# Moving the end of VectorE's order in the dense expert loop: gates ahead of rows in the last 16 steps

## The reference

```python
top_s, top_pos = lax.top_k(cand_s, PEER_TOPK)
experts = jnp.take_along_axis(cand_i, top_pos, axis=-1)
g = jax.nn.softmax(top_s, axis=-1)
u = peer_u[experts]
act = jax.nn.gelu(jnp.einsum('thkd,td->thk', u, xb), approximate=False)
v = peer_v[experts]
return jnp.einsum('thk,thkd->td', g * act, v)
...
y = layer_norm(ALPHA * h + ff, ln2_g, ln2_b)
```

## Time and profile before

| | us |
|---|---|
| median of 3 runs | 3522.22 |
| lowest and highest run | 3514.46, 3530.64 |
| profiled execution, its own time | 3518.77 |
| its span in the profile | 3517.0 |
| PE busy | 3031.8 |
| VectorE busy | 2456.1 |
| ScalarE busy | 1205.2 |
| GpSimd busy | 1549.8 |

### The profile page before, as it was taken

How to read it: one execution, slowest core, us unless ns; L and a number is a source line. 1 busy time by engine, 2 the same in 40 slices (tenths; PEclk the granted TensorE clock), 3 DMA queues, 4 the chain that set the end, 5 groups by cost and what they waited for, 6 DMA issues and landing times. The chain is left out here.

```text
span 3517.0 us, 36218 instructions
## 1 busy us (share of the span) xinstructions
PE 3031.8 (86%) x10170; PEld 1718.4 (49%) x10170; DVE 2456.1 (70%) x5185; ACT 1205.2 (34%) x3180; POOL 1549.8 (44%) x1186
## 2 busy tenths in 40 slices
PE   8979989776889896776886899999998999999996
PEld 5755745444645453444653554444444444444442
DVE  0122068887786878877767677888878888788887
ACT  0241233665543435764552322222222222222221
POOL 0000035567562288888777533233333333334331
PEclk9989999886799998886697999999999999999998
DMA  4665589666699997576578999999999999999996
GB/s 145 210 252 187 173 325 375 235 194 202 215 340 374 336 347 232 150 197 173 168 252 295 404 411 394 410 403 406 406 398 397 414 407 402 384 411 415 408 401 245
DMA packets 375914, 1098.52 MB, mean 312 GB/s; under 512 B 91713, under 2 KB 210209, under 8 KB 289569
## 3 DMA queue, kind: packets, MB, share of 16 engines
q0 software_dynamic: 165072, 751.05, 57.1%
q1 hardware_dynamic: 176800, 303.85, 24.6%
q10 hardware_dynamic: 33840, 41.30, 3.3%
HBM read 1031.97 MB, written 63.02 MB: 311 GB/s over the span
## 5 line engine op out<-in xcount | busy, mean ns | idle before, releaser
L428 POOL DMA_INDIRECT expert_rows<-in_experts,picked_index x640 | 769.6, 1202 | 1254.7 <-DVE ff_sum L583 1142.6
L571 DVE SCALAR_TENSOR_TENSOR expert_rows<-expert_rows,h_tile 128x1024 f32<-128x1024 f32 x672 | 819.2, 1219 | 244.6 <-DMA expert_rows<-in_experts,picked_index 218.1
L583 DVE SCALAR_TENSOR_TENSOR ff_sum<-expert_rows,coefficients,ff_sum 128x1024 f32<-128x1024 f32 x672 | 859.8, 1279 | 139.5 <-ACT coefficients L534 138.0
L1792 PE MATMUL dense_act_ps<-dense_hT,key_columns 128*128 128x384 f32 x2048 | 705.3, 499 | 114.5 <-DMA key_columns<-in_key_columns 103.6
L451 POOL DMA_INDIRECT gates_by_expert<-dense_gate,gate_address x384 | 673.8, 1755 | 156.7 <-issue 124.5
L1781 PE MATMUL dense_out_ps<-dense_value_rows,dense_weights 128*128 128x512 f32 x1536 | 682.5, 595 | 17.9 <-DVE dense_weights L1860 17.9
L1792 PEld LDWEIGHTS dense_act_ps<-dense_hT,key_columns 128*128 128x128 f32 x2048 | 389.1, 194 | 450.4 <-DMA key_columns<-in_key_columns 180.0
L1781 PEld LDWEIGHTS dense_out_ps<-dense_value_rows,dense_weights 128*128 128x128 f32 x1536 | 292.9, 191 | 362.5 <-issue 310.6
L839 PE MATMUL proj_ps<-xT,w_in_block 128*128 128x384 f32 (+1 forms) x1392 | 422.0, 466 | 36.1 <-PEq L1601 15.5
L839 PEld LDWEIGHTS proj_ps<-xT,w_in_block 128*128 128x128 f32 x1392 | 267.8, 193 | 189.4 <-issue 35.6
L1826 ACT ACTIVATE dense_weights<-dense_act_ps 128x384 f32<-128x384 f32 x128 | 62.6, 489 | 742.5 <-PE dense_act_ps L1792 730.9
(11 more groups left out here) (189 smaller groups left out, 3088.2 us busy)
## 6 DMA issues: line engine op xcount, KB each, us to landing
key_columns<-in_key_columns SPq DMA_DIRECT2D x128, 512.0 KB, 11.6
dense_value_rows<-in_experts SPq DMA_DIRECT2D x128, 512.0 KB, 8.2
gates_by_expert<-zeros POOLq DMA_DIRECT2D x12, 2048.0 KB, 21.9
wq_half<-in_peer_wq SPq DMA_DIRECT2D x48, 512.0 KB, 12.6
dense_gates<-gates_by_expert SPq DMA_DIRECT2D x128, 192.0 KB, 12.1
w_in_block<-in_w_in ACTq DMA_DIRECT2D x18, 1024.0 KB, 9.8
w_in_block<-in_w_in SPq DMA_DIRECT2D x18, 1024.0 KB, 8.1
w_out<-in_w_out SPq DMA_DIRECT2D x24, 512.0 KB, 7.8
```

The costliest lines, as they stand in the source:

```text
L428: pool.indirect_dma_start(to, None, self.a["experts"], bass.IndirectOffsetOnAxis(ap=index[:, k:k + 1], axis=0)).then_inc(self.got[p % self ...
L571: dve.scalar_tensor_tensor(place, place, 1.0, self.h[n % 2][:], ALU.mult, ALU.mult, accum_out=self.dots[:, s % TOPK:s % TOPK + 1]).then_in ...
L583: dve.scalar_tensor_tensor(total, self.ring[:, p % self.RING, D:2 * D], self.coef[:, y % TOPK:y % TOPK + 1], total, ALU.mult, ALU.add).the ...
L1792: mm = nc.tensor.matmul(up[it % 2][:, 0:W], keys[it % KB][:, k, :], hTd[:, k, :], start=(k == 0), stop=(k == KC - 1))
```

## The change

In the last 16 steps VectorE takes the gates earlier: `ahead` grows from 2 to 6 tiles over the steps 121 to 124 (two gates in each of them), so that the last gate stands in step 129 and not in step 133. SyncE loads the gates earlier in the same measure. And the function `part` has a larger divisor (259, before 253): in every step before 130 a smaller share of the background list is due. Step 130 takes it to 0.985, step 131 to the end (before: step 132).

```diff
-        LAG, AHEAD = 8, 2
+        LAG, CATCH_UP = 8, 16
...
-        part = lambda it: min(1.0, (min(it + 1, ET) + max(0, it + 1 - LAG)) / (2 * ET - 3))
+        ahead = lambda it: 2 + min(4, max(0, it - (ET + LAG - CATCH_UP)))
+        weighed = lambda it: min(ET, max(0, it - LAG + ahead(it) + 1))
+        part = lambda it: ((min(it + 1, ET) + max(0, it + 1 - LAG)) / (2 * ET + 3) if it < ET + LAG - 6 else
+                           0.985 if it == ET + LAG - 6 else 1.0)
...
-                e = it - LAG + 4
-                if 0 <= e < ET:
+                for e in range(weighed(it + 1), weighed(it + 2)):
                     if e == 0:
                         wait_for_scores(sp, m, len(GROUPS))
...
                     sp.dma_start(gts[e % GB][:], gates_of[e]).then_inc(gts_in[e % GB], 16)
+                e = it - LAG + 4
+                if 0 <= e < ET:
                     if e >= VB:
                         sp.wait_ge(v_filled, e - VB + 1)
                     sp.dma_start(vals[e % VB][:], table[e][:, D:2 * D]).then_inc(vals_in[e % VB], 16)
...
-                e = it - LAG + AHEAD
-                if 0 <= e < ET:
+                for e in range(weighed(it - 1), weighed(it)):
                     dve.wait_ge(gelud, e + 1)
                     dve.wait_ge(gts_in[e % GB], 16 * (e // GB + 1))
                     nc.vector.tensor_tensor(w[e % AB][:], w[e % AB][:], gts[e % GB][:], ALU.mult).then_inc(gated, 1)
```

## The result

| | before | after |
|---|---|---|
| median us | 3522.28 (4 runs) | 3566.33 (4 runs, 3563.41 to 3571.28) |
| ratio | 1 | 1.012, 95% interval 1.010 to 1.014 |
| span in the profile | 3517.0 | 3561.7 |

The change makes the kernel 44 us slower. The forecast was 3526 us, +3.5, with 3544 as the upper end of its range.

The account below looks back on a forecast made before the run. Bytes moved were taken to bound the loop, with rows tied to TensorE. Last gelu 3430, plus 46 and 44.5, gave a 3520.5 us span, +3.5 against 3517.0; median 3526, range 3508 to 3544.

Parts of the forecast that it names:

- What bounds the kernel: Dense loop: bound by bytes moved, DMA share 1.00 at 404 GB/s; VectorE's rows cannot run ahead of TensorE.
- Part 3, the gate loads: SyncE's queue, last dense steps: early gate loads could hold back key columns, but don't while VectorE is at TensorE's step.
- the 10.35 us of that part: VectorE waiting for tile 124's gelu before its gate: costs at most one TensorE step if cover is gone.
- Part 2, the divisor: Rows near the loop's end: 24 coefficients stand behind the last dense gelu, moving the last row's dot product to 3476.
- g: End of the last dense gelu on ScalarE: 3443.1 us before, forecast 3430.
- rival 1: TensorE gains nothing because keys still land in 12 us: last dense gelu stays 3443, +15.5 to +19.5 us; chance 20%.
- X - g: From last dense gelu's end (g) to start of the last row's dot product (X) on VectorE: forecast 46 us.
- byte count: Data still to move after the last dense gelu: 20.4 MB, at about 415 GB/s 49 us.
- VectorE's own chain: VectorE's remaining rows 653 to 671 and two gates after the last dense gelu: 45 us at the earliest.
- Part 1, the tail: No gates behind the last row, sample sums sooner after it: worth 3.5 us, 7.3 at most.
- End minus X: From the last row's dot product to the kernel's end: 48 us before, forecast 44.5, floor 40.7; h load kept at 8.8.
- a DMA share clearly under 1: Sign that the forecast is wrong: in the loop, fetches starved by the held rows.

Follow-up runs that it names:

- e12: Gates up to six tiles ahead, 10 gate buffers, old divisor 253, coefficients one dense gelu earlier, against the kernel before: 3505.77 us, 0.9940.
- e5: The whole change (divisor 259) with 10 gate buffers and coefficients one dense gelu earlier, against the kernel before: 3519.52 us, 0.9979.
- e3: The whole change with 10 gate buffers instead of 4, against the kernel before: 3531.77 us, 1.0027.
- e4: Gates up to six tiles ahead with 10 gate buffers, divisor and end of part of before, against the kernel before: 3517.03 us, 0.9986.
- e1: The change's divisor and end of part alone, gates two tiles ahead, 4 gate buffers, against the kernel before: 3546.8 us, 1.0067.
- e6: Gates up to six tiles ahead, 10 gate buffers, divisor 247, against the kernel before: 3509.82 us, 0.9960.

## Why the prediction was wrong

**What bounds the kernel**: right as far as it goes. The DMA share is 1.00 as long as all sides run, and rows are tied to TensorE through ScalarE's coefficients; loosening that tie by a step pays 0.46 to 0.48% at either divisor (e12, e5).

**Part 3, the gate loads: the step that failed.** The prediction named the danger and dismissed it: SyncE's gate loads "could hold back the key columns queued behind; they don't while VectorE is at TensorE's step". But SyncE works a step ahead of TensorE: before, it issues the gates of its step 126 at 3409.93 us, and TensorE begins its fill of step 125 at 3410.76. For SyncE, VectorE "at TensorE's step" is late. Before, SyncE's step needs only gates that VectorE does two steps earlier. With two gate loads per step and 4 buffers, in its step 122 it needs the gates of tiles 117 and 118, which VectorE does in its own step 122: the slack is gone. The trace of before had a warning, the 56.4 us that this queue waits for VectorE from 3300 to 3480 us. I had looked at each wait alone, at times taken from before, and not followed the ring round. It cost 0.93% (after against e3), about 33 of the 44 us, and was priced at nothing; the 10.35 us of that part were for VectorE's own waits for a gelu.

**Part 2, the divisor**: the direction was right and its size too small, 14 us (e3 against e4) where 7 was forecast (the +3.5 with the 3.5 of the tail taken off). Two terms were off. The first is g, forecast 3430: with the ring cut (e3) it is 3437.3, a gain of 6 and not 13 us. Only half of that is a TensorE that gets its keys sooner: its last fill starts 2.9 us earlier (3431.43, before 3434.34), while the key waits up to 3440 us fell from 103.6 to 91.7; in e4, with the old divisor, they are 96.5. The rest is a fill of 5.32 us instead of 7.12 and a gelu that no longer waits for its turn on ScalarE. In e1 the last fill starts 2.1 us later than before. So rival 1 (TensorE gains nothing) was nearly right on g.

The second is X - g, forecast 46: it is 57.0 in e3 and 57.1 after the change. The prediction's own byte count gave 49, of which it used only 46. In e3 22.15 MB are moved from g to X (expected 20.4) at a mean of 389 GB/s (expected 415). VectorE's own chain was to be 45 us, and the waits for fetches in that stretch, priced at 1 us, are 10.3. The rate is low in e3 too, where no load had been held up. In the windows from g to X, first e3, then the change:

```profile
3437.00:3455.00 18.00, 18.00 (x43) 7.98 (x42) 16.08 (x21) 5.20 (x23) 7.27 (x6) 1.00 0.97 374
3455.00:3475.00 20.00, 13.35 (x26) 5.20 (x25) 12.36 (x17) 2.49 (x10) 4.68 (x5) 0.83 1.01 374
3475.00:3494.00 19.00, 17.46 (x41) 7.41 (x39) 17.21 (x22) 3.48 (x14) 5.86 (x6) 1.00 1.01 418
```

```profile
3462.00:3480.00 18.00, 18.00 (x44) 7.96 (x43) 16.00 (x21) 5.41 (x23) 7.28 (x6) 1.00 0.80 308
3480.00:3500.00 20.00, 13.51 (x26) 5.08 (x25) 12.29 (x17) 2.44 (x10) 4.70 (x5) 0.83 1.02 371
3500.00:3520.00 20.00, 17.81 (x42) 7.60 (x40) 18.03 (x23) 3.54 (x15) 6.15 (x6) 1.00 1.00 413
```

Most of this time the share is near 1 and still the engines move 371 or 374 GB/s; why is open. With the two measured terms the sum for e3 is 3437.3 + 57.0 + 42.4 = 3536.7, its span.

**Part 1, the tail**: right. End minus X was to be 44.5 and at least 40.7; it is 42.0, since h took 6.1 us from the sample sums' end (3532.5) to the first of the last tiles, not 8.8. (In e4, with the old end of `part`, it is 46.2.) TensorE's waits for gates went, and were worth nothing, as said. The gates' whole gain with enough buffers is 0.14% (e4), forecast 3.5 us, measured 5, not clear of zero.

**The rivals**: none had the ring. For rival 1 I drew on the Trainium skill, DMA: Bandwidth & Descriptors, Queues, rings and completion order (round-robin between queues that have work). The runs lie near its strict reading, by which g would stay 3443: with the divisor 259 and no ring the last fill starts 2.9 us earlier than before (e3) or 2.1 us later (e1), where bytes would allow 16 to 19. The 15 to 20 us that rival 1 put on the time came in e3's profile (+19.7 us of span) for another reason in part, the 57 us from g to X.

**What would have shown it**: of the signs listed, "a DMA share clearly under 1" is what came, 0.92 and 0.75.

## What to carry to other kernels

When a load is moved earlier in an in-order queue, every wait in front of it moves too: write down for each who must have done what, in which step of its own, and follow that releaser back until it ends or comes round to the queue itself. Here the ring, without a step of slack in it, made the keys 11.3 and 13.4 us late in two steps, close to the 12.0 us that a key load takes; with two more buffers at one link the cost was gone, and with a step of slack at another link two thirds of it. A constant that paces a background list against the main loop has an optimum with a loss each way (with gates ahead and 10 buffers: best at 247, 0.26% worse at 253, and 0.7% worse at 241 and at 259, the latter with its new end of `part`). Whether it has to be set again when a tie between the engines is loosened was not tried. And an experiment that takes a cost away shows its cause only if the same edit does nothing where that cost is absent: e5 alone seemed to settle how the divisor costs, and e12 took it back.

## What the runs showed that was not expected

Ten runs of the same kernel can differ by 16 us in this program (e6: 3504.95 to 3521.26), so effects of 5 us need many runs, and a profile taken at the upper end of that spread (e6's 11 us above its median, e12's 7) shows a difference of a few us only with that doubt. And one line that moves ScalarE's coefficients a step ahead pays 0.46 to 0.48% at either divisor, though at the old divisor VectorE's waits for coefficients do not fall at all (31.6 and 33.1 us).
